# An encoder layer with a mixture of experts: order of the late loads and of the closing work

## What is computed

```python
x = layer_norm(ALPHA * x + mixer(x, ...), ln1_g, ln1_b)
scores = sigmoid(x @ w_router)          # 16 experts in 4 groups; one group, the best two in it
h = silu(x @ w_gate[e]) * (x @ w_up[e]) # D_EXPERT = 256
y = sum over the two of gate * (h @ w_down[e])
shared = (silu(x @ ws_gate) * (x @ ws_up)) @ ws_down
x = layer_norm(ALPHA * x + y + shared, ln2_g, ln2_b)
```

## Time and profile before

| what | us |
|---|---|
| median of 3 runs | 1216.82 (1216.77 to 1220.33) |
| profiled execution, its own time | 1218.3 |
| its span, first to last instruction | 1216.4 |
| PE busy | 1200.7 (99%) |
| DVE busy | 724.8 (60%) |
| ACT busy | 591.5 (49%) |
| POOL busy | 218.7 (18%) |

### The profile page before, as it was taken

How to read it: one execution, slowest core, us unless ns; L and a number is a source line. 1 busy time by engine, 2 the same in 40 slices (tenths; PEclk the granted TensorE clock), 3 DMA queues, 4 the chain that set the end, 5 groups by cost and what they waited for, 6 DMA issues and landing times.

```text
span 1216.4 us, 22118 instructions
## 1 busy us (share of the span) xinstructions
PE 1200.7 (99%) x8040; PEld 1077.8 (89%) x8040; DVE 724.8 (60%) x1796; ACT 591.5 (49%) x1463; POOL 218.7 (18%) x276
## 2 busy tenths in 40 slices
PE   9999999999999999999899999999999999999998
PEld 9998888888888888888778888899989999999895
DVE  3222455655565556555767878668856556656358
ACT  4332344544454445444552434244556756766556
POOL 1121001200120012001211122000224423432223
PEclk9999999999999999999989999999999999999999
DMA  9787674365436643667745333493899999999994
GB/s 274 225 302 227 155 196 101 79 165 136 101 80 153 149 101 79 156 164 217 259 140 220 124 122 125 162 360 124 265 335 286 286 287 264 282 295 272 350 311 188
DMA packets 164676, 246.93 MB, mean 203 GB/s; under 512 B 41536, under 2 KB 111424, under 8 KB 163776
## 3 DMA queue, kind: packets, MB, share of 16 engines
q1 hardware_dynamic: 149408, 190.72, 51.5%
q0 software_dynamic: 11776, 41.95, 14.0%
q10 hardware_dynamic: 3408, 13.16, 2.7%
HBM read 150.59 MB, written 65.31 MB: 177 GB/s over the span
## 4 chain that ended last, share of the span: by engine, by line
PE 71%; issue 13%; DVE 5%; DMA 5%; POOL 3%; ACT 1%; POOLq 1%; ACTq 0%; SPq 0%; DVEq 0%
PE bank L916 15%; PE bank L918 15%; PE bank L917 15%; PE bank L1049 9%; PE bank L1036 5%; PE bank L1027 4%; PE bank L1028 3%; PE bank L910 3%; DMA raw_gu<-in_w_up 2%; DMA acc_scratch<-slab,dstc 1%; POOL c_work L2527 1%; DVE w_gu_lo L2180 1%; DVE c_work L2073 1%; DVE c_work L2071 1%; POOL Q L2554 1%
## 5 line engine op out<-in xcount | busy, mean ns | idle before, releaser
L1523 ACT ACTIVATE b_work<-b_work 128x256 f32<-128x256 f32 (+3 forms) x288 | 148.1, 514 | 232.6 <-DVE b_work L1976 232.5
L916 PE MATMUL bank<-xgT_hi,w_gu_hi 128*128 128x224 f32 (+1 forms) x704 | 195.8, 278 | 0.9 <-DVE xgT_lo L2031 0.5
L918 PE MATMUL bank<-xgT_hi,w_gu_lo 128*128 128x224 f32 (+1 forms) x704 | 194.8, 277 | 0.0
L917 PE MATMUL bank<-xgT_lo,w_gu_hi 128*128 128x224 f32 (+1 forms) x704 | 194.7, 277 | 0.0
L1985 DVE COPY b_work<-bank 128x256 f32<-128x256 f32 (+2 forms) x256 | 112.7, 440 | 117.3 <-PE bank L1036 116.3
L916 PEld LDWEIGHTS bank<-xgT_hi,w_gu_hi 128*128 128x128 f32 x704 | 135.0, 192 | 3.2 <-DVE xgT_lo L2031 1.4
L917 PEld LDWEIGHTS bank<-xgT_lo,w_gu_hi 128*128 128x128 f32 x704 | 135.0, 192 | 0.7
L918 PEld LDWEIGHTS bank<-xgT_hi,w_gu_lo 128*128 128x128 f32 x704 | 135.0, 192 | 0.0
L2554 POOL CAST Q<-Q 128x512 fp32r<-128x512 f32 x48 | 53.4, 1143 | 431.5 <-DVE w_k_lo L1915 225.8
L1036 PE MATMUL bank<-keep,b_work 128*128 128x128 f32 x608 | 114.7, 274 | 3.1 <-ACT b_work L1523 3.1
L1036 PEld LDWEIGHTS bank<-keep,b_work 128*128 128x128 f32 x608 | 79.4, 139 | 36.4 <-ACT b_work L1523 7.8
(11 more groups left out here) (247 smaller groups left out, 2831.6 us busy)
## 6 DMA issues: line engine op xcount, KB each, us to landing
raw_gu<-in_w_gate SPq DMA_DIRECT2D x32, 512.0 KB, 8.8
raw_gu<-in_w_up SPq DMA_DIRECT2D x32, 512.0 KB, 9.6
raw_d<-in_w_down SPq DMA_DIRECT2D x16, 1024.0 KB, 9.7
Q<-stage_hi SPq DMA_DIRECT2D x96, 128.0 KB, 2.4
Q<-stage_lo SPq DMA_DIRECT2D x96, 128.0 KB, 2.4
o_scratch<-b_work SPq DMA_DIRECT2D x36, 264.0 KB, 3.3
wo_scratch<-a_work POOLq DMA_DIRECT2D x16, 512.0 KB, 4.6
w_o<-wo_scratch SPq DMA_DIRECT2D x16, 512.0 KB, 5.8
```

Of the source, the lines that this page charges most:

```text
L916: nc.tensor.matmul(o, w_hi, x_hi, start=first, stop=False)
L917: nc.tensor.matmul(o, w_hi, x_lo, start=False, stop=False)
L918: return nc.tensor.matmul(o, w_lo, x_hi, start=False, stop=last)
L1523: nc.scalar.activation(prob[:, u % 2, 0:n], prob[:, u % 2, 0:n], ACT.Exp, scale=-1.0, bias=o[:, HD:HD + 1], accum_out=o[:, HD + 1:HD + 2])\
```

## The change

- **Loads.** Late rows 0 are loaded ahead of the shared gate and up weights, and not behind them. `ln2_g` and `ln2_b` are loaded ahead of late rows 1. Late rows 2 come after row tiles 0 to 3, and not right after late rows 1. Row tiles come in the order 0 to 11.
- **Late step 0.** The last routed step's down products come after the first group of gate products and not the second; their first half waits for the low down weights quarter by quarter.
- **Last down products** go to banks 2, 3 and 0, 1, and wait for the gated product (`hx_made`) and not for the evictions of the step before.
- **Offset.** High and low part of `ln2_b` stand on the two halves of the partitions, with two stacked identities as weights: one product per bank and not two.
- **Three tiles on TensorE** (8, 9, 10) and not four; tile 7 is normalized on VectorE.
- **Placing.** Statistics and normalizations of tiles 1, 2 and 3 move into late step 1; those of 4 and 5 into the last; each scale copy follows its own tile's statistics.

The diff, cut to its core:

```diff
@@ -366,17 +366,18 @@
-Z_ORDER = (0, 1, 2, 3, 4, 6, 7, 5, 8, 9, 10, 11)
+Z_ORDER = tuple(range(TILES))
 Z_BN, Z_ACT = Z_ORDER[0:1], Z_ORDER[1:]
...
-Z_PE = (7, 8, 9, 10)
+Z_PE = (8, 9, 10)
 Z_DVE = tuple(t for t in Z_ORDER if t not in Z_PE)
...
-b_hi, b_lo = (gu1[1][:, D * c:D * c + D] for c in range(2))
-ident_r = gu1[1][:, 2 * D:2 * D + P]
+b_two = gu1[1][:, 0:D]
+both = gu1[1][:, 2 * D:2 * D + P]
 zdiag = tail_t[:, 0:len(Z_PE) * P].rearrange("p (t c) -> p t c", c=P)
@@ -502,6 +503,10 @@
+LAST_DOWN = (bank[2:4], bank[0:2])
+Z_BANKS = (bank[4:6], bank[6:8], bank[2:4])
 def half_rows(n, half):
@@ -859,37 +864,41 @@
+    def load_late(n):
+        for part in range(2):
+            sp.dma_start(plain(xg_of(LATE0 + n)[part][:]), t_d[n, part]).then_inc(S[f"late_ld{n}"], 16)
     with sp.Fori(0, more * 2 + 3) as j:
...
+    sp.wait_ge(S["gx_made"], EARLY + 2)
+    load_late(0)
     for half in range(2):
...
-    def load_late(n):
-        for part in range(2):
-            sp.dma_start(plain(xg_of(LATE0 + n)[part][:]), t_d[n, part]).then_inc(S[f"late_ld{n}"], 16)
-    sp.wait_ge(S["gx_made"], EARLY + 2)
-    load_late(0)
     load_d(more * 2 + 3)
-    wait("gx_made", more * 2 + (EARLY + 4))
-    load_late(1)
-    load_late(2)
-    wait("wd_lo", more * 8 + 20)
-    load_raw_d(ws_down)
     wait("wg_lo", (more * 2 + 6) * KD)
...
     sp.dma_start(ln2b, ln2_b.partition_broadcast(P)).then_inc(S["ln2_loaded"], 16)
+    wait("gx_made", more * 2 + (EARLY + 4))
+    load_late(1)
+    wait("wd_lo", more * 8 + 20)
+    load_raw_d(ws_down)
...
     acc_t = acc_d.rearrange("(t p) d -> t p d", p=P)
-    wait("gx_made", more * 2 + (EARLY + 5))
     for t in Z_ORDER:
+        if t == 4:
+            load_late(2)
+        if t == 2 * EARLY + 2:
+            wait("gx_made", more * 2 + (EARLY + 5))
         sp.dma_start(base[:, t, :], acc_t[t]).then_inc(S[f"rows_ld{t}"], 16)
@@ -1253,21 +1262,27 @@
-    def ddn(q, s, half, n):
+    def ddn(q, s, half, n, by_parts=False, banks=None):
...
             pe.wait_ge(S["h_lo"], q + 1)
-            if n == 0 or EARLY <= n <= LATE0:
+            if (n == 0 or EARLY <= n <= LATE0) and not by_parts:
                 pe.wait_ge(S["wd_lo"], 4 if n == 0 else (q - (EARLY - 2)) * 4)
-        if n > 0:
+        if banks is not None:
+            pe.wait_ge(S["hx_made"], q + 1)
+        elif n > 0:
             pe.wait_ge(S["y_read0" if half == 0 else "y_read1"], q)
...
         rows = half_rows(n, half)
+        o = bank[4 + 2 * half:6 + 2 * half] if banks is None else banks
         for k in range(2):
             for c in range(2):
+                if by_parts:
+                    pe.wait_ge(S["wd_lo"], (q - (EARLY - 1)) * 4 + (2 * k + c + 1))
                 a, b = s * 512 + k * 256 + half * P, k * D + 512 * c
-                last = three(bank[4 + 2 * half + c][0:rows, :], h_hi[:, a:a + rows], h_lo[:, a:a + rows],
+                last = three(o[c][0:rows, :], h_hi[:, a:a + rows], h_lo[:, a:a + rows],
                              wd_hi[:, b:b + 512], wd_lo[:, b:b + 512], k == 0, k == 1)
@@ -1296,9 +1311,9 @@
-            if f == 1:
+            if f == 0:
                 for half in range(2):
-                    ddn(q - 1, 1 - s, half, n - 1)
+                    ddn(q - 1, 1 - s, half, n - 1, half == 0)
@@ -1380,34 +1395,32 @@
     for half in range(2):
-        ddn(end, LATE % 2, half, LATE0 + LATE - 1)
+        ddn(end, LATE % 2, half, LATE0 + LATE - 1, False, LAST_DOWN[half])
...
             pe.wait_ge(S["b_ready"], 1)
-        if n >= 2:
-            pe.wait_ge(S[f"y_read{n - 2}"], end + 1)
+        pe.wait_ge(S["y_read1" if n == 1 else "y_read0"], end + 1 if n == 2 else end)
         for c in range(2):
-            for part in (b_hi, b_lo):
-                nc.tensor.matmul(bank[2 * n + c][:], ident_r, part[:, 512 * c:512 * c + 512],
-                                 start=part is b_hi, stop=False)
+            nc.tensor.matmul(Z_BANKS[n][c][:], both, b_two[:, 512 * c:512 * c + 512],
+                             start=True, stop=False)
...
         for c in range(2):
-            nc.tensor.matmul(bank[2 * n + c][:], zdiag[:, n, :], base[:, t, 512 * c:512 * c + 512],
+            nc.tensor.matmul(Z_BANKS[n][c][:], zdiag[:, n, :], base[:, t, 512 * c:512 * c + 512],
                                     start=False, stop=True).then_inc(S["z_summed"], 1)
...
     offsets(2)
-    offsets(3)
     for n in range(1, len(Z_PE)):
         scaled_rows(n, Z_PE[n])
@@ -1781,8 +1794,11 @@
             act.wait_ge(S["ln2_loaded"], 32)
-            copy(ident_r, ident)
-            copy(b_hi, ln2b).then_inc(S["b_split"], 1)
+            for h in range(2):
+                own = slice(HD * h, HD * h + HD)
+                copy(both[own, :].rearrange("p (a c) -> p a c", a=2),
+                     ident[own, own].unsqueeze(1).to_broadcast([HD, 2, HD]))
+            copy(b_two, ln2b).then_inc(S["b_split"], 1)
         if soon:
@@ -1801,13 +1817,15 @@
             z_stats(1)
+            z_stats(2)
         if last:
-            for t in (3, 4, 6, 7):
+            for t in (5, 6, 7):
                 z_stats(t)
...
         if n == LATE0 + 1:
-            z_stats(2)
+            z_stats(3)
+            z_stats(4)
         if not soon and EARLY <= n < LATE0 - 1:
@@ -1869,20 +1887,18 @@
             act.wait_ge(S["z_summed"], 2 * n + c + 1)
-            last = copy(base[:, t, 512 * c:512 * c + 512], bank[2 * n + c][:])
+            last = copy(base[:, t, 512 * c:512 * c + 512], Z_BANKS[n][c][:])
         last.then_inc(S["fin_act"], 1)
...
-    for t in (5, 8):
-        z_stats(t)
+    z_stats(8)
     scales(0, Z_PE[0])
...
     z_stats(11)
-    scales(3, Z_PE[3])
     for n, t in enumerate(Z_PE):
@@ -2199,7 +2215,8 @@
             sums = zpart[:, 2 * tile + half, c:c + 1] if tile >= EARLY else None
-            last = V.scalar_tensor_tensor(b, bank[4 + 2 * half + c][:], 1.0 / ALPHA, b, ALU.mult, ALU.add,
+            made = LAST_DOWN[half] if tile == EARLY + LATE - 1 else bank[4 + 2 * half:6 + 2 * half]
+            last = V.scalar_tensor_tensor(b, made[c][:], 1.0 / ALPHA, b, ALU.mult, ALU.add,
                                           accum_out=sums)
@@ -2226,22 +2243,25 @@
         if last:
-            for t in (2, 3, 4):
-                z_out(t)
+            z_out(4)
+            z_out(5)
         if n == LATE0 + 1:
             dve.wait_ge(S["b_split"], 1)
-            V.tensor_tensor(b_lo, ln2b, plain(b_hi), ALU.subtract).then_inc(S["b_ready"], 1)
+            V.tensor_tensor(b_two[HD:P, :], ln2b[HD:P, :], plain(b_two[HD:P, :]), ALU.subtract)\
+             .then_inc(S["b_ready"], 1)
         if soon:
...
             z_out(0)
+            z_out(1)
+            z_out(2)
         gated(q, s, n)
+        if n == LATE0 + 1:
+            z_out(3)
         if last:
             z_centre_half(6, 0)
-        if n == LATE0 + 1:
-            z_out(1)
         if rows:
@@ -2496,9 +2516,8 @@
     z_scale_half(6, 0)
+    z_scale_half(6, 1).then_inc(S["fin_ready"], 1)
     add_shared(end - 1, EARLY + LATE - 2, 1)
-    z_scale_half(6, 1).then_inc(S["fin_ready"], 1)
-    add_shared(end, EARLY + LATE - 1, 0)
@@ -2506,10 +2525,10 @@
-    z_centre(7)
+    z_out(7)
+    z_centre(8)
+    add_shared(end, EARLY + LATE - 1, 0)
     add_shared(end, EARLY + LATE - 1, 1)
-    z_out(5)
-    z_centre(8)
     z_centre(9)
```

## The result

| what | before | after |
|---|---|---|
| median of the runs beside each other, us | 1217.28 (6 runs, 1216.09 to 1220.33) | 1225.36 (6 runs, 1223.76 to 1227.64) |
| ratio to before | | 1.0069, 95% interval 1.0057 to 1.0081 |
| profiled execution, its own time, us | 1218.3 | 1226.74 |
| its span, us | 1216.4 | 1224.9 |

The change made the kernel 8.4 us slower (0.0069 x 1217.28). The prediction said slower, by 4.0 us, with a range up to 1223.5: the direction held, the size did not.

What follows compares the result with a forecast made beforehand. The prediction took the end as bound by scatters delaying the row loads, then VectorE's list and ScalarE's tail. Row loads at 1165.8 plus 54.6 gave span 1220.4, +4.0; added to the median 1216.82: 1220.8 us, range 1214.0 to 1223.5.

Steps and rivals of the forecast that it cites:

- S: Time SyncE issues the first row load near the end: 1166.45 before, forecast 1165.8, set by two scatters in a row.
- S + 54.6: The sum for the end of the span: first row load, VectorE's list, ScalarE's tail, evictions and store; 1220.4 us.
- rival 4: Shared gate and up weights land after about 1140.3 and TensorE stands; landing at 1141.5 gives +1.2, 1222 us; chance 0.04.
- 1147.3 + 5.5 + 3.4: Landing of the second scatter before the last routed step's: start, lone pair, other queue's packets (1.44 MB); 1156.2.
- The list from S: VectorE's work from the row loads to tile 10's sums, 26.0 us from 1180.4 to 1206.4, then ScalarE's tail.
- ScalarE's waits for GpSimd: Three waits for reciprocal roots before the scale copies, 1.4 to 1.9 us each as sign; 1.8 taken for tile 10.
- Tile 7 on VectorE: A centring of 1.22 us becomes a whole normalization of 2.6 to 2.75 us on VectorE's list: +1.4 us.
- TensorE's closing products: Offset and scaled products at the end shrink from 10.8 to 6.7 us; if they alone decided, end at 1211.2.
- Late rows 2: Land at S + 14.8 (1180.6); TensorE stands 3.5 us before gate products, at no cost because VectorE's list covers it.
- 1: Rival: scatters get free, S at 1161.1 to 1164.5, end 1215.7 to 1219.1, within 0.3% of before; chance 0.38.
- 2: Rival: TensorE's closing products set the end, not VectorE's list; 1211.2, 5.2 us faster; chance 0.12.
- rival 3: TensorE's stand for late rows 2 lowers its clock; ends 3.4 us later, 1.4 beyond the cover: 1222.2; chance 0.06.

Runs made afterwards that it cites:

- e1: Changed kernel with late rows 0 loaded behind the shared gate and up weights again; ratio to before 1.0019.
- e12: e11 with late rows 0 ahead of the shared gate and up weights, as in the changed kernel; ratio to before 1.0008.
- e10: e1 with the vectors (`ln2_g`, `ln2_b`) loaded behind the shared down weights again; ratio to before 1.0004.
- e11: e9 with the vectors (`ln2_g`, `ln2_b`) loaded behind the shared down weights again; ratio to before 0.9985.
- e5: e1 with each of ScalarE's three scale copies one tile later, behind the next tile's statistics; ratio to before 1.0014.
- e9: e6 with tile 7's two banks evicted by VectorE, not ScalarE, and the tile stored by SyncE; ratio to before 0.9994.
- e4: Kernel before with the changed kernel's order of loads and nothing else, so the old tail; ratio to before 1.0047.
- e3: Changed kernel with all loads in the order of before, so the new tail alone; ratio to before 1.0045.
- e6: e5 with tile 7 back on TensorE as a fourth tile; ratio to before 1.0009.
- e8: e1 with tile 7 back on TensorE, each scale copy still at once (tile 7's behind tile 8's statistics); ratio to before 1.0036.
- the square: e1, e5, e8, e6: three or four tiles on TensorE, scale copy at once or one tile later; first row load to end 54.21, 52.76, 54.69, 52.08 us.
- e7: Kernel before, old tail, with vectors and late rows 2 moved as in the change, late rows 0 left behind the weights; ratio to before 1.0006.
- e2: Changed kernel with late rows 2 loaded right behind late rows 1 again; ratio to before 1.0073.

## Why the prediction was right or wrong

**The start of the row loads is the step that failed.** The prediction put S at 1165.8, "only 0.65 us earlier"; it came at 1170.08, 3.6 later than before and 4.3 later than forecast. That is the whole error: S + 54.6, its own sum, gives 1224.7, and the span is 1224.9. The 4.3 us are 1.5 in the issue of the scatter, 2.1 in its time to land and 0.7 in what follows up to S, where the last scatter took 0.9 longer. Inside the step:

- The late landing of the shared gate and up weights was seen and nearly sized (1137.7; it was 1138.66). It was priced for TensorE alone, as rival 4, with a need by 1140.3. What else stands behind the split was put at nothing without a reason: ScalarE's rows for the scatters do, in the same list. So "the scatters start at about 1147.5" and the landing at "1147.3 + 5.5 + 3.4" kept the issue of before; it moved by 1.5 us. e1 and e12 show this link from both sides.
- The same wait holds SyncE, for the vectors. The prediction had them issued near 1140.5 and late rows 1 half done when the scatters start; late rows 1 were only issued at 1142.96. So the scatter took 12.97 us where 10.9 was forecast, and the last scatter 7.12, 0.9 more. Counting packets of both queues was the right method, with a start 2.5 us off. e10, e11 and e12 show the size: the scatter takes 5.9 us beside little, 8.2 with late rows 0 first, 9.4 to 10.5 with the vectors first (e1, e5 to e9), 13.0 with both moves (e4 and the changed kernel).
- Of the three moves of the loads, one was good. Late rows 2 out of the scatters' way gives 4.0 us of S - A (53.00 in e3 to 49.01 in e10), the early vectors take back 1.9, late rows 0 in front 2.4 by themselves and 5.2 together with the vectors (50.88 to the 56.05 of e4 and the changed kernel).

**The list from S held in its total.** Sums of tile 10 at S + 40.2 (forecast S + 40.6), evictions from S + 46.4 (46.5), last eviction's end S + 50.5 (50.6). e3, which has the new tail with the loads of before, needs 54.0. Inside it two errors partly cancel, and that is luck: the normalization of tile 2 began at S + 13.0 where S + 14.6 was forecast, and the work from there to the sums of tile 10 took 27.2 us for 26.0, with 0.6 us of it a wait for TensorE.

**ScalarE's waits for GpSimd** came as forecast in number and releaser. In size they were 1.09, 2.45 and 2.11 us, all three outside the 1.4 to 1.9 that the prediction names as the sign; the one in the sum, for tile 10, was 1.8 and 0.1 for the handing over there. GpSimd's powers for tiles 8 to 11 in the changed kernel (start, us, instruction):

```profile
1203.99 0.55 POOL L2692 TENSOR_TENSOR keep<-keep 128x1 f32<-128x1 f32 x1
...
1207.96 1.48 POOL L2692 TENSOR_TENSOR keep<-keep 128x1 f32<-128x1 f32 x1
...
1212.80 1.48 POOL L2692 TENSOR_TENSOR keep<-keep 128x1 f32<-128x1 f32 x1
...
1216.93 0.55 POOL L2692 TENSOR_TENSOR keep<-keep 128x1 f32<-128x1 f32 x1
```

The second and third run beside centrings, whose rows and gain both lie in SBUF; the first beside an addition of a bank, the last with VectorE idle. The rule of the Trainium skill, page "SBUF — State Buffer", section "Who interferes with whom", separates them in just this way (two inputs in SBUF block GpSimd's reads, one doesn't), and the trace agrees: 1.48 us against 0.55. The copies' place is the dearest part of the new tail that a run isolates: 1.45 us (e5), 2.6 with four tiles (e6 against e8).

**Tile 7 on VectorE, priced at +1.4,** is mis-sized as a net price. The 1.4 us of VectorE's list are real, but the eviction that ScalarE no longer makes is worth about as much: the square gives +0.7 and -0.5 us. The prediction counted VectorE's side, and ScalarE's side only as three evictions in the sum, so it never showed as a trade.

**TensorE's closing products** no longer set the end, as the sum had it; and its last down products didn't wait for banks. Worth on the path: e6 against e7 is 1.6 us of end - S, but e7's stand and lost clock are in that, so what the other banks and the one-product offset bring by themselves stays open; no run has them alone.

**Late rows 2** were forecast to land at S + 14.8 and to make TensorE stand 3.5 us, at no cost. They landed at S + 12.8 (1182.90), TensorE stood 4.14 us since S itself was later, and with the clock it cost at most the 0.65 us of e2. The reason, that VectorE's list covers it, holds for this tail. "Gone that cover (S early), so is the stall" holds where S is early (no stand in e10 and e11, with S at 1163.1 and 1161.6), but the cover can also go with the tail: in e7 stand and clock come to 3.7 us.

**The rivals.** 1 (the scatters get free, S at 1161.1 to 1164.5) happened as soon as the two bad moves were undone: S - A 49.0 in e10 is 1162.7 on before's scale. It was the other moves that prevented it, not the packet count given against it. 2 didn't occur. 3, given 0.06, happened in its mechanism: the clock fell, by 3.45 us where 3.4 was estimated from the earlier trace rows, but 0.65 us with the stand reached the end, not 1.4. That the sizes agree is luck: in e4 a stand of 3.4 us cost 1.7 us of clock. The 0.95 in the earlier trace rows, which rival 3 passes over, lies behind TensorE's last product: from 1201 to 1211.7 the clock is 1.00. By the rule of the Trainium skill, page "TensorE: Matmul & The Clock Gate", Part 1, a wait for a transfer can lower the clock, and here the trace agrees, with the 0.50 of 1183 to 1188. 4 named the right load; but TensorE, for which it was priced, had its first gate product without waiting (1143.27), and the cost went over ScalarE and SyncE.

## What to carry to other kernels

When a load comes later, list everything behind the wait on each engine that waits for it, not only the engine that uses the data: here TensorE, the weights' user, didn't wait for them at all, and the scatter rows queued behind them on ScalarE, and a load queued behind them on SyncE, were what cost. "In order of need" has to count the transfers that other queues issue: a load moved out of the scatters' time pays, a load moved in front of it pushes the next one into it. And when a wait at the end goes from one engine's list to another's, count the second engine's list to its last store too.

## What the runs showed of the hardware

- An issue on SyncE isn't free when its queue is loaded. The same issue of 512 KB (the first piece of the second half of the weights) held SyncE for 6.2 to 6.7 us in all four kernels that had 2.1 MB of late rows in front of it (changed, e2, e4, e12), and for 1.5 to 2.5 in the ten others. In the changed kernel that put off the next issue by 4.4 us against before (1125.15 to 1120.80).
- TensorE's clock behind a stand on a load: after 1.4 us (e5) it stayed at 1.00 in every row, after 2.0 us (e7) it read 0.80 and 0.77 in rows of 4 us, after 3.4 us (e4) 0.69 and 0.88, after 4.1 us (changed) 0.50 and 0.89 in rows of 5 us. The loss came to 1.7, 1.7 and 3.45 us, from half to nearly all of the stand again.
- A scatter's time to land depends mostly on what else is in the queues: 5.9 to 13.9 us for the same transfer over these kernels.
